# Hybrid decoder layer on one core: the memory projection placed behind the first feed-forward stage

## The reference, cut to what matters

```python
x = x + 0.5 * post1(SwiGLU_1(pre1(x)))          # D_FF = 5632
x = x + postm(W_out concat[norm_a(DilatedSWA), norm_b(StickBreaking), norm_m(MemCross)])
x = x + 0.5 * post2(SwiGLU_2(pre2(x)))

def memory_kv(mem, g_mem, w_mem_kv):            # mem (1, 256, 2048), w_mem_kv (2048, 1024)
    k, v = jnp.split(rms_norm(mem, g_mem) @ w_mem_kv, 2, axis=-1)
```

## Time and profile before

| what | value |
|---|---|
| runs | 2297.71, 2304.29, 2305.02 us; median 2304.29 |
| profiled execution | 2313.5 us |
| its span in the trace | 2311.7 us (1.8 us lie around it) |
| TensorE busy with matmuls | 2171.0 us, 94% of the span |
| VectorE, ScalarE, GpSimd busy | 59%, 39%, 20% |
| mean granted TensorE clock | 0.968 |

### The profile page before, as it was taken

How to read it: one execution, slowest core, us unless ns; L and a number is a source line. 1 busy time by engine, 2 the same in 40 slices (tenths; PEclk the granted TensorE clock), 3 DMA queues, 4 the chain that set the end, 5 groups by cost and what they waited for, 6 DMA issues and landing times.

```text
span 2311.7 us, 41524 instructions
## 1 busy us (share of the span) xinstructions
PE 2171.0 (94%) x16875; PEld 2060.2 (89%) x16875; DVE 1374.7 (59%) x3226; ACT 908.3 (39%) x1146; POOL 459.0 (20%) x400
## 2 busy tenths in 40 slices
PE   7999999999999997989877779889999999999997
PEld 7899999999999997989862228889999999999996
DVE  6665555555555567687694326485555555555556
ACT  3343444343443445334231413454343444343443
POOL 4420000000000015568610110350000000000004
PEclk9899999999999998999988998999999999999998
DMA  7355555555555553988998995445555555555551
GB/s 275 110 188 187 177 180 181 182 183 183 180 178 177 179 182 128 334 300 315 324 288 289 301 220 184 164 146 183 182 178 177 178 180 182 183 180 185 179 178 47
DMA packets 221537, 459.26 MB, mean 199 GB/s; under 512 B 11466, under 2 KB 12363, under 8 KB 220571
## 3 DMA queue, kind: packets, MB, share of 16 engines
q1 hardware_dynamic: 219874, 452.32, 59.3%
q0 software_dynamic: 1472, 4.29, 0.5%
HBM read 447.95 MB, written 8.62 MB: 198 GB/s over the span
## 4 chain that ended last, share of the span: by engine, by line
PE 46%; DVE 5%; DMA 3%; SPq 2%; issue 1%; POOL 1%; ACT 0%; POOLq 0%; DVEq 0%; ACTq 0%
PE ps L490 14%; PE ps L492 14%; PE ps L491 14%; DMA v_cache<-win_v 2%; DVE k_cache L1340 2%; SPq L415 1%; PE ps L762 1%; PE ps L642 1%; DVE head_space L1340 1%; SPq L414 1%; POOL acc L1622 1%; DMA v_cache<-sb_v 1%; POOL xT L1629 1%; DVE swap L1319 0%; DVE qT L1320 0%
## 5 line engine op out<-in xcount | busy, mean ns | idle before, releaser
L1146 DVE TENSOR_TENSOR wl<-raw,wh 128x1024 fp32r<-128x1024 f32 x592 | 731.8, 1241 | 708.6 <-ACT wh L842 707.9
L490 PE MATMUL ps<-xh,wh 128*128 128x264 f32 (+1 forms) x3840 | 1100.7, 287 | 28.0 <-DVE xl L1158 16.7
L842 ACT ACTIVATE wh<-raw 128x1024 fp32r<-128x1024 f32 x656 | 692.2, 1059 | 1056.4 <-PE ps L492 1056.3
L492 PE MATMUL ps<-xh,wl 128*128 128x264 f32 (+1 forms) x3840 | 1097.1, 286 | 0.0
L491 PE MATMUL ps<-xl,wh 128*128 128x264 f32 (+1 forms) x3840 | 1097.1, 286 | 0.0
L490 PEld LDWEIGHTS ps<-xh,wh 128*128 128x128 f32 x3840 | 729.0, 190 | 31.0 <-issue 19.8
L492 PEld LDWEIGHTS ps<-xh,wl 128*128 128x128 f32 x3840 | 729.0, 190 | 0.0
L491 PEld LDWEIGHTS ps<-xl,wh 128*128 128x128 f32 x3840 | 728.6, 190 | 0.0
L490 PE MATMUL ps<-hh,wh 128*128 128x264 f32 x1408 | 400.8, 285 | 0.0
L492 PE MATMUL ps<-hh,wl 128*128 128x264 f32 x1408 | 399.9, 284 | 0.0
L491 PE MATMUL ps<-hl,wh 128*128 128x264 f32 x1408 | 399.1, 283 | 0.0
(11 more groups left out here) (218 smaller groups left out, 1133.3 us busy)
## 6 DMA issues: line engine op xcount, KB each, us to landing
raw<-w_gu SPq DMA_DIRECT2D x176, 1024.0 KB, 5.1
raw<-w_down SPq DMA_DIRECT2D x88, 1024.0 KB, 5.1
raw<-w_in SPq DMA_DIRECT2D x40, 1024.0 KB, 7.2
v_cache<-sb_v SPq DMA_DIRECT2D x128, 256.0 KB
k_cache<-sb_k SPq DMA_DIRECT2D x84, 256.0 KB
raw<-w_out SPq DMA_DIRECT2D x16, 1024.0 KB, 5.4
head_space<-sb_k SPq DMA_DIRECT2D x44, 256.0 KB
raw<-w_mem_kv SPq DMA_DIRECT2D x8, 1024.0 KB, 9.5
```

Source lines behind the costliest of these rows:

```text
L490: pe.matmul(out, w_hi, rh(k0 + kk), start=first and kk == 0, stop=False)
L492: mm = pe.matmul(out, w_lo, rh(k0 + kk), start=False, stop=last and kk == 1)
L842: act.activation(wh[:, c % UNIT_SLOTS], raw_unit(c), ACT.Copy).then_inc(hi_made, 1)
L1146: dve.tensor_tensor(wl[:, c % UNIT_SLOTS], raw_unit(c), wh[:, c % UNIT_SLOTS].bitcast(F32), ALU.subtract).then_inc(lo_made, 1)
```

## The change

- The order of the stages becomes: first feed-forward stage, memory projection, mixer. The kernel starts with the transposes of `x` (now over 8 banks) and the weights of the feed-forward stage. VectorE makes unit 0 and the first two `xl` tiles before units 1 and 2.
- The memory's rows are loaded behind the first four weight chunks, in pieces of 512 bytes (`mem_space`). Their squares are summed by ScalarE along the row with `accum_out` (2 instructions, 128x2048), in the first phase. Root, inversion and scaling of the rows (2 instructions, 128x2048, in place) follow by step 1. In steps 2 to 5 TensorE transposes 8 blocks each time, before the sixth unit of up, and ScalarE copies the 4 tiles back (`take_memory`). `xh` and `xl` of the memory are made in the last step, when `xh` is free.
- The memory projection comes as 8 pairs of units: one for the keys as before (24 matmuls, 256 columns), one for the values with the tokens stationary and the weights streaming (12 matmuls, 512 columns, `value_unit`), whose results are rows already. The scaling at lines 1199 and 1203 is gone, and so are the 8 transposes of the values.
- The work of the join stands between the splits of these 16 units: the partition sum after 4 units, all 16 scalings of `y` on VectorE, GpSimd's additions, and the first 4 of 8 pairs of `xh` and `xl` for the mixer.
- Then 4 copies of the keys and 2 of the values on VectorE, and 8 transposes of the keys (`turn_memory_keys`) behind the mixer's first unit. The squares for the mixer's norm come four at a time in the first half of its first 16 units.
- GpSimd stores the memory's rows behind the mixer's squares; key tiles 0 and 1 of the mixer wait for `xl_ready["mem"]`.

```diff
-CH_MEM = 0
-CH_FFN1 = CH_MEM + 8
-CH_IN = CH_FFN1 + 12 * FF_STEPS
+CH_FFN1 = 0
+CH_MEM = CH_FFN1 + 12 * FF_STEPS
+CH_IN = CH_MEM + 8
...
+            for t in range(2):
+                sp.dma_start(mem_space[:].rearrange("p k (t n) -> p k t n", t=2)[:, :, t],
+                             mem_prompt[0, P * t:P * t + P].rearrange("p (k n) -> p k n", k=KT)
+                             ).then_inc(mem_loaded, 16)
...
+            def turn_memory(part):
+
+                pe.wait_ge(mem_scaled, 2)
+                pe.wait_ge(g_read[0], 4 * (part + 2) + 4)
+                for k in range(4 * part, 4 * part + 4):
+                    for t in range(2):
+                        mm = pe.transpose(ps[k % 4][:, P * t:P * t + P], mem_space[:, k, P * t:P * t + P], ident[:])
                     mm.then_inc(mem_turned, 1)
...
+            def value_unit(c):
+
+                v, slot = u_mem + 2 * c + 1, (2 * c + 1) % UNIT_SLOTS
+                pe.wait_ge(lo_made, v + 1)
+                for t in range(2):
...
+                        pe.matmul(out, x_hi, wh[:, slot, kk], start=c == 0 and kk == 0, stop=False)
+                        pe.matmul(out, x_hi, wl[:, slot, kk], start=False, stop=False)
+                        mm = pe.matmul(out, x_lo, wh[:, slot, kk], start=False, stop=c == 7 and kk == 1)
...
+            for c in range(8):
+                pe.wait_ge(xl_ready["mem"], 2 * c + 2)
+                if c == 2:
+                    sum_partitions("post1", 6)
+                unit(u_mem + 2 * c, (2 * c) % UNIT_SLOTS, lambda k: xh[:, k, 0:N_MEM], lambda k: xl[:, k, 0:N_MEM],
+                     2 * c, 0, N_MEM, c == 0, c == 7, memk_done,
+                     lambda j: pe.wait_ge(y_added[0], 16 * FF_STEPS + 8 + j + 1))
+                value_unit(c)
...
-            pe.wait_ge(rooted, nth("post1"))
-            two_groups(u_in, TOK, (0, 4), (in_done, in_done), (None, None), xl_ready["mix"],
-                       lambda: sum_beside("mix"))
+            two_groups(u_in, TOK, (0, 4), (in_done, in_done), (lambda j: pe.wait_ge(memk_read, j + 1), values_read),
+                       xl_ready["mix"], lambda: sum_beside("mix"), turn_memory_keys)
...
+            u_mem, u_in = unit_of(CH_MEM), unit_of(CH_IN)
+            for c in range(8):
+                split(u_mem + 2 * c + AHEAD)
+                if c == 3:
+                    update_pair("mix", 0, G_POST1)
+                    update_pair("mix", 1, G_POST1)
+                if c in (4, 5):
+                    update_pair("mix", 2 * c - 4, G_POST1)
+                if c >= 4:
+                    lower_pair("mix", c - 4, G_PREM)
+                split(u_mem + 2 * c + 1 + AHEAD)
+                if c == 2:
+                    invert("post1", r_post)
+                    dve.wait_ge(r_ready, nth("post1"))
+                if c == 3:
+                    update_pair("mix", 2, G_POST1)
+                    update_pair("mix", 3, G_POST1)
+                if c in (4, 5):
+                    update_pair("mix", 2 * c - 3, G_POST1)
+            for j in range(4):
+                block_ready(j, memk_done, 0, u_mem + 14)
+                dve.tensor_copy(memkT[:, j], ps[j][:, 0:N_MEM]).then_inc(memk_read, 1)
```

More of the change, by code:

```diff
@@ L391, in _ @@
             ffn(0, CH_FFN1)
+            for n in range(8):
+                load_pair(CH_MEM + n, n, w_mem_kv[0], slice(0, 2))
             win_ = w_in[0].rearrange("(k p) n -> p k n", p=P)
@@ L495, in unit, with group, two_groups @@
                 mm.then_inc(unit_used, 1)
-            def group(v, width, bank, done, guard, ready=None):
+            def group(v, width, bank, done, guard, between=None):
                 for c in range(8):
-                    if ready is not None:
-                        pe.wait_ge(ready, 2 * c + 2)
+                    if c == 5 and between is not None:
+                        between()
                     unit(v + c, c % UNIT_SLOTS, lambda k: xh[:, k, 0:width], lambda k: xl[:, k, 0:width],
                          2 * c, bank, width, c == 0, c == 7, done, guard)
-            def two_groups(v, width, banks, done, guard, ready, between):
+            def two_groups(v, width, banks, done, guard, ready, between, turn=None):
                 for c in range(8):
@@ L509, in two_groups @@
                     for n in range(2):
+                        if c == 0 and n == 1 and turn is not None:
+                            turn()
                         if c == 7 and n == 1:
@@ L530, in _ @@
             pe.transpose(ps[7][:, 0:P], gain_rows[:], ident[:]).then_inc(gains_turned, 1)
-            pe.wait_ge(mem_loaded, 32)
+            pe.wait_ge(gains_ready, 1)
+            pe.wait_ge(rows_loaded, 48)
             for k in range(KT):
[L533 to L553, removed]
+                if k >= 8:
+                    pe.wait_ge(turn_read, k - 7)
+                out = ps[(k + 4) % 8]
                 for t in range(2):
@@ L576, in u_guard @@
                         pe.wait_ge(y_added[l], s * 16 + (j + 1 - 4))
+                    memory = l == 0 and 2 <= s < 6
                     group(v, TOK, 0, g_done[l], g_guard)
-                    group(v + 8, TOK, 4, u_done[l], u_guard)
+                    group(v + 8, TOK, 4, u_done[l], u_guard, between=(lambda: turn_memory(s - 2)) if memory else None)
+                    if memory:
+                        pe.wait_ge(mem_turn_read, 4 * (s - 2) + 4)
                 def down(i, par, v, end=False):
@@ L1178, in _ @@
                 dve.wait_ge(turned, k + 1)
-                dve.tensor_copy(xT[:, k, 0:N_MEM], ps[k % 4][:, 0:N_MEM]).then_inc(turn_read, 1)
+                dve.tensor_copy(xT[:, k], ps[(k + 4) % 8][:, 0:TOK]).then_inc(turn_read, 1)
             dve.wait_ge(gains_ready, 1)
-            for c in range(AHEAD):
-                split(c)
             def lower_pair(name, c, gain):
@@ L1250, in ffn @@
                     bring_in(1)
+                else:
+                    split(0)
                 lower_pair(name, 0, gain)
@@ L1253, in ffn @@
                     bring_in(2)
+                else:
+                    split(1)
+                    split(2)
                 lower_pair(name, 1, gain)
@@ L1655, in _ @@
             tiles = list(range(KT))
-            squares("mem", xT, tiles, lambda k: pool.wait_ge(turn_read, k + 1), width=N_MEM)
-            pool.wait_ge(turned, 2 * KT)
+            pool.wait_ge(turned, KT)
             pool.memset(y[:], 0.0).then_inc(y_added[0], 16)
-            squares("ffn1", xT, tiles, lambda k: pool.wait_ge(turn_read, KT + k + 1), before="mem")
-            pool.wait_ge(mem_rows_made, 4)
-            for t in range(2):
-                store(nmk_p[0, 0, P * t:P * t + P].rearrange("s h d -> s (h d)"), mem_out[:, t], mem_stored)
-                store(nmv_p[0, 0, P * t:P * t + P].rearrange("s h d -> s (h d)"), memv[:, t], mem_stored)
+            squares("ffn1", xT, tiles, lambda k: pool.wait_ge(turn_read, k + 1))
             def ffn(l):
@@ L1722, in _ @@
             update("end")
+            pool.wait_ge(mem_stored, 16 * 4)
             pool.wait_ge(stored, 16 * 6)
```

213 lines of the change are left out of this document (133 added, 80 removed).

## The result

| | before | after |
|---|---|---|
| runs of this comparison | 2296.13 to 2305.02 us, median of four 2301.00 | 2274.75 to 2277.51 us, median of four 2276.43 |
| profiled execution, its span | 2313.5, 2311.7 us | 2277.14, 2275.3 us |
| mean granted TensorE clock | 0.968 | 0.978 |

What follows compares the result with a forecast made beforehand. TensorE, busy for 2171.0 of 2311.7 us, was taken to bound the kernel. Terms -71.2 + 7.4 + 34.3 + 1.6 - 1.0 = -28.9 us from the median 2304.3 gave 2275.4 us, range 2262 to 2293.

Steps and rivals of the forecast that it cites:

- Start: Kernel start to first feed-forward matmul: at 22.0 us instead of 93.22, so -71.2 us.
- The unknown is the transposes' clock: At the start: whether the 16 tiles of x run at full clock; taken as 0, kept at 0 to +5.1 us.
- DMA at the start: Memory's 2 MB in 512-byte packets ahead of weight chunk 4: chunk lands near 30 us, wanted near 39; cost 0.
- In the stage: First feed-forward stage: 32 added transposes +6.4, scaling of the memory's rows +0.8, root and inversion 0.2; in all +7.4 us.
- Join: Stage end (T) to mixer, now with the memory projection: mixer at T + 49.1 instead of 14.8, VectorE last; +34.3 us.
- Behind it: Behind the mixer's start: 8 transposes of keys +1.6 us, the vanished wait for the squares -1.0 us.
- The sum: Whole kernel: -71.2 + 7.4 + 34.3 + 1.6 - 1.0 = -28.9 us, forecast 2275.4 us.
- Blocked fully: Rival, join: GpSimd slows every VectorE tile to 0.995, mixer at 55.1 after T; 2281 us; chance 0.13.
- Keeps up: Rival, join: VectorE keeps up, mixer at 44.7 after T, no clock drop; 2268 us; chance 0.13.
- Weights late: Rival, start: weight chunk 4 comes late, +10 us, 2285 us; chance 0.07.
- not hidden: Rival, stage: at each of 4 turns a split and four copies (2.8) show, +11 us, 2287 us; chance 0.05.
- Slower: Rival, value projection: 512-column matmuls miss one column a cycle; no gain from 0.525 each, 2356 us at 1.07; chance 0.05.

Runs made afterwards that it cites:

- combined: Changed kernel with `xs_rows` loaded first, 28 unused matmuls around the transposes of x, memory squares earlier, three `xl` pairs behind the key and value copies; 2269.56 us, ratio 0.9853.
- after_again: The changed kernel run once more, unchanged; 2278.88 us (median of six), ratio to before 0.9891.
- warm_mm: Changed kernel plus 20 unused float32 matmuls of 128 columns ahead of the wait for the rows of x; 2275.82 us, a single run.
- warm_tr: Changed kernel plus 20 unused transposes ahead of the wait for the rows of x; 2279.14 us, a single run.
- lower_late: Changed kernel with three of the mixer's four early `xl` pairs made behind the key and value copies; 2281.65 us, ratio to before 0.9864.
- join_serial: Changed kernel with the projection moved, but the join's sum, root, scaling, additions and splits in series behind its 16 units; 2283.28 us, ratio to before 0.9899.
- values_turned: Changed kernel with values projected like keys, weights stationary, 24 matmuls of 256 columns a unit, then 8 more transposes; values came out wrong; 2282.99 us, ratio to before 0.989.

## Why the prediction was right

**Start: -66.5 instead of -71.2; the failing term.** "The unknown is the transposes' clock ... so I take 0 and keep 0 to +5.1." It was the upper end: 16 tiles at 0.82 are 13.1, not 8.0. What failed is the reading of 6.41 us for the memory's 32 transposes as full pace. Full pace is 0.109 each, and 26 of the 32 ran at 0.213, as slow as those of x did here. The price of one, 0.20, looked right beside a tile of x at 0.50, but such a tile has another form, with a small transpose between the large ones: 0.50 is its full pace and 0.82 its half. The row of the same form (the transposes of x themselves, at 0.52 of full clock from 77 us on the earlier trace rows) was the right one. A transfer landed 0.8 later than taken, as `xs_rows` came last, 11.04 for 10.2. The last piece was over-priced: 2.5 from the last tile to the first matmul, not 3.8, since one split and two `xl` tiles had no other engine beside them. 0.8 + 5.1 - 1.3 = 4.6, and 4.7 is missing. Why the clock rose under the memory's transposes and not under those of x stays open.

**DMA at the start: right about the end, wrong about the queue.** TensorE never waits for weights in the first units. But SyncE spends 11.85 us issuing the memory's two transfers, and chunk 4 is issued at 28.59 (timeline of SyncE's queue, changed kernel):

```profile
9.51 11.85 SPq L364 DMA_DIRECT2D mem_space<-mem_prompt  x2
...
28.59 0.62 SPq L345 DMA_DIRECT2D raw<-w_gu  x1
```

**In the stage: +5.65 instead of +7.4.** The transposes cost less: at full clock they start 0.109 apart, 3.5 us for 32, where I had priced them from the earlier trace rows at 0.20 each, which was mostly half pace (timeline of TensorE; the end is modelled):

```profile
187.57 1.03 PE L563 MATMUL ps<-ident,mem_space 128*128 128x128 f32 x8
```

No wait stands behind them, and none behind the scaling (3.88 on ScalarE), for which I had taken 0.8. What I had put at 0.2, root and inversion, cost 0.87: in step 0 TensorE waits 2.02 for its banks, in the kernel before 1.15. ScalarE and VectorE in the changed kernel:

```profile
72.40 1.06 ACT L889 ACTIVATE wh<-raw 128x1024 fp32r<-128x1024 f32 x1
73.47 1.28 ACT L915 ACT_TABLE_LOAD   x1
74.77 0.47 ACT L915 ACTIVATE root<-ps,eps 128x248 f32<-128x248 f32 x1
...
75.43 1.80 DVE L1262 RECIPROCAL r_pre<-root 128x264 f32<-128x264 f32 x1 [0.72 <-ACT root L916]
77.27 0.17 DVE L1346 RECIPROCAL mem_r<-mem_r 128x2 f32<-128x2 f32 x1
```

Before, the memory's norm had already loaded the root's table, and the root in step 0 followed the split at once. Now its load of 1.28 stands in the chain, VectorE waits 0.72 for it, and the memory's inversion adds 0.17: 0.89. This is read from the rows; combined, which moved the squares and kept the load, still waited 2.02, so the squares are not the cause. A term that the sum does not have at all comes on top: behind this wait the clock fell, and 15 matmuls went at 0.22 instead of 0.12 (the stretch from 77.80 under combined), 1.5 us. Behind the wait of 1.15 in the kernel before it did not fall. Together 3.5 + 0.9 + 1.5 are 5.9, against 5.65 measured.

**Join: +34.0, forecast +34.3.** The mechanism was as described: TensorE done first, VectorE last with the key copies, GpSimd's additions stretching its tiles (busy 0.66 and 0.76 a tile against my 0.67 and 0.93). Two errors cancel in VectorE's chain: the ten splits took 14.3 instead of 12.1, since four of them met additions, which I had not priced, and the eight `xl` tiles 6.1 instead of 7.4. For TensorE, a value unit is 12 x 0.231 = 2.77, not 2.69, so twice the 256-column pace (0.235) was nearer, and with a wait of 0.5 for a split TensorE ended 1.5 later than the 44.7; VectorE came 0.3 earlier. The idle time was 2.54 instead of 4.4. The clock did not fall in after; it did in after_again, warm_mm and warm_tr, at 1.3 to 1.5 instead of 2.6.

**Behind it: -1.8, forecast +0.6.** The wait for the squares (-1.0) is gone, and the gap behind the units is 1.09 longer: late next was not ScalarE but VectorE's chain of inversion and scaling (1.8 + 1.45 + 1.44), which had run ahead while TensorE waited. The 8 transposes cost 0.9, 0.109 apart, not 1.6. The rest of the 16 units' -2.87, some -2.7, is the clock: the drop of the old join, which I had priced at 2.6 and forecast as no difference, did not come in this execution. In after_again it came, shorter, and the -1.8 is only -0.5.

**The sum.** -66.5 + 5.65 + 34.0 - 1.8 = -28.65 against -28.9. That this is so close is luck: 4.7 too much at the start against 1.8 in the stage and 2.4 behind the join, and of these 2.4 the clock at the mixer gives and takes 1.3 from one execution to the next (the whole is -26.9 in after_again).

**The rivals.** "Blocked fully" fell by its number and not by its mechanism. Each tile that met an addition took 0.98 to 1.00, just as between 893 and 930 us, but only 12 of the 24 met one; with all of them the mixer would have come at T + 55 to 57, and it came at 48.75. "Keeps up" needed 44.7; lower_late came to 46.46 by moving six tiles. "Weights late" and "not hidden" had no wait to show, but for the 0.87. "Slower": 0.231 against a turning point of 0.525.

## What to carry to other kernels
Independent work that stands alone at the start is worth moving beside a join whose chain leaves TensorE idle: here the move paid by running start and norm once instead of twice, and the bare move already hid most of the chain (join_serial lost only some 4 to 5 us). TensorE's first work in a program, transposes and matmuls alike, should be priced at the pace of the lower clock level; 20 unused matmuls in the idle time before the data brought the first feed-forward matmul forward by 4.3 us. A row is a price only for its own form and its own clock, so take the pace of neighbouring instructions from their starts before using it. When a first user of a ScalarE function is moved, its table load goes to whoever comes next: look whether that one is on the chain.

## What the runs showed that was not expected
- The clock column says 1.00 from 11 to 29.7 us of the changed kernel, while transposes (0.82 a tile) and matmuls (0.22) run at the pace of the lower level. There is no record of the clock yet; the matmuls' starts are the better clock.
- 11 us of transposes without a pause (12 to 23 us of warm_tr) ran at 0.50, and yet transposes alone had raised the clock at 8.64 us of the same execution and at 15.60 us of the kernel before.
- VectorE's tiles took 0.48 or 0.98 us beside GpSimd, never a value between; the mean of 0.70 describes none of them.
- The same gap of 2.5 us ahead of the mixer brought the clock down in three of four executions whose join is alike, and it fell within 3 us behind the same wait of 2.0 us in step 0 in six of eight.
- Two accumulations that share a bank: the second's start lost the first's earlier part (values_turned).
- The part behind the last mark, the same code everywhere, spread over 12.5 us between executions.
